# Moving tiles of the dense stages begin 32 bytes off the weights' tiles

## The reference

```
z = rms_norm(x) @ w_in;  zf, zq, zk, zv, zm = split(z)
y = concat(fourier(zf), window_attention(zq, zk, zv), memory_attention(zm, mem))
x = x + rms_norm(group_norms(y) @ w_out)
gate, up = split(rms_norm(x) @ w_ffn_in)          # 2 x 2816 channels
x = x + rms_norm((silu(gate) * up) @ w_ffn_out)
```

```
x = x + 0.5 * swiglu(rms_norm(x), ffn1_w1, ffn1_w2)
proj = rms_norm(x) @ w_in + b_in
x = x + (g0 * y_a(proj) + g1 * y_b(proj) + g2 * y_c(proj)) @ w_out
x = x + 0.5 * swiglu(rms_norm(x), ffn2_w1, ffn2_w2)
```

## Time and profile before

| | us | share |
|---|---|---|
| median of three runs | 3464.14 | |
| profiled execution, span | 3464.2 | |
| TensorE matmuls | 3364.4 | 97% |
| TensorE weight loads (beside matmuls) | 2886.5 | 83% |
| VectorE | 2451.1 | 71% |
| ScalarE | 1628.3 | 47% |
| GpSimd | 67.0 | 2% |

### The profile page before, as it was taken

The page is one execution under the profiler, slowest core; times in us unless marked ns, Lnnn a source line. Parts: engine busy times, 40 slices in busy tenths (PEclk is TensorE's granted clock), DMA queues, the critical chain, the costliest instruction groups (busy, mean ns, idle before and its releaser), DMA issues. The chain is left out here.

```text
span 3464.2 us, 49516 instructions
## 1 busy us (share of the span) xinstructions
PE 3364.4 (97%) x19557; PEld 2886.5 (83%) x19557; DVE 2451.1 (71%) x3500; ACT 1628.3 (47%) x2399; POOL 67.0 (2%) x96
## 2 busy tenths in 40 slices
PE   7999999999999999999999999999999989999999
PEld 5679988768998899887678899889988757788997
DVE  8669854759872988467885698458864888658863
ACT  4645643445652556335523365336542562335642
POOL 1000000000000000000000000000000000000000
PEclk9999999999999999999999999999999999999999
DMA  4123323213332333232132333333333212223332
GB/s 141 50 73 110 110 87 110 92 44 92 110 110 97 92 106 115 94 101 65 54 97 86 98 106 102 101 106 108 101 104 108 71 49 85 85 97 98 110 104 85
DMA packets 341371, 325.25 MB, mean 94 GB/s; under 512 B 31960, under 2 KB 312356, under 8 KB 341156
## 3 DMA queue, kind: packets, MB, share of 16 engines
q1 hardware_dynamic: 335588, 307.95, 28.0%
q0 software_dynamic: 3776, 12.45, 1.6%
q10 hardware_dynamic: 1792, 1.88, 0.2%
HBM read 313.84 MB, written 2.10 MB: 91 GB/s over the span
## 5 line engine op out<-in xcount | busy, mean ns | idle before, releaser
L2168 DVE TENSOR_TENSOR w_lo<-raw,w_hi 128x2048 fp32r<-128x2048 f32 x190 | 435.2, 2291 | 482.7 <-ACT w_hi L1524 482.4
L1524 ACT ACTIVATE w_hi<-raw 128x2048 fp32r<-128x2048 f32 x190 | 363.8, 1915 | 835.5 <-PE products L799 582.7
L799 PE MATMUL products<-a_hi,w_hi 128*128 128x512 f32 (+1 forms) x1216 | 489.6, 403 | 12.1 <-DVE a_lo L2228 9.5
L799 PE MATMUL products<-a_hi,w_lo 128*128 128x512 f32 (+1 forms) x1216 | 476.3, 392 | 0.0
L799 PE MATMUL products<-a_lo,w_hi 128*128 128x512 f32 (+1 forms) x1216 | 475.5, 391 | 0.0
L940 PE MATMUL products<-seven_x,w_hi 128*128 128x256 f32 x2592 | 464.5, 280 | 2.4 <-DVE w_lo L2467 2.3
L940 PEld LDWEIGHTS products<-seven_x,w_hi 128*128 128x128 f32 x2592 | 395.0, 188 | 4.1 <-DVE w_lo L2467 3.6
L940 PE MATMUL products<-seven_x,more_hi 128*128 128x256 f32 x1632 | 376.1, 280 | 5.6 <-ACT rs_b L1636 5.6
L940 PE MATMUL products<-seven_x,w_lo 128*128 128x256 f32 x1296 | 361.5, 279 | 0.0
L799 PEld LDWEIGHTS products<-a_hi,w_hi 128*128 128x128 f32 (+1 forms) x1216 | 229.3, 189 | 69.0 <-issue 16.5
L940 PEld LDWEIGHTS products<-seven_x,more_hi 128*128 128x128 f32 x1632 | 277.5, 188 | 6.8 <-ACT rs_b L1636 6.8
(11 more groups left out here) (465 smaller groups left out, 7242.8 us busy)
## 6 DMA issues: line engine op xcount, KB each, us to landing
raw<-in_ffn_w SPq DMA_DIRECT2D x244, 512.0 KB, 4.2
raw<-in_w_in SPq DMA_DIRECT2D x108, 512.0 KB, 4.6
raw<-in_w_ffn_in SPq DMA_DIRECT2D x88, 512.0 KB, 4.3
raw<-in_w_ffn_out SPq DMA_DIRECT2D x40, 512.0 KB, 4.5
raw<-in_w_out SPq DMA_DIRECT2D x32, 512.0 KB, 4.0
raw<-in_ffn_w SPq DMA_DIRECT2D x24, 384.0 KB, 3.6
x_sums<-x_sums POOLq DMA_DIRECT2D x12, 512.0 KB, 5.9
raw<-in_w_mem_kv SPq DMA_DIRECT2D x8, 512.0 KB, 3.9
```

Of the source, the lines that this page charges most:

```text
L799: mm = pe.matmul(G[pair][0:m, into + b, 0:n], w[:, s, at:at + m], x, start=(first or into > 0) and k == 0 and q == 0, stop=(last or ends) ...
L1524: act.activation(w_hi[:, s, :], raw[:, s, :], ACT.Copy).then_inc(hi_ready, 1)
L2168: dve.tensor_tensor(w_lo[:, s, :], raw[:, s, :], w_hi[:, s, :].bitcast(F32), ALU.subtract).then_inc(lo_ready, 1)
```

## The change

Three constants ODD_A, ODD_H and ODD_Y, all 32, move tiles:

- `a_hi` and `a_lo` begin 32 bytes behind their old places; the region's length is written out, so that REGION_B stays where it was.
- `h_hi`, `h_lo` and `h_full` (which shares h_lo's bytes) begin 32 bytes later; h_lo's region is 1 KB longer. The early weight forms of the block products, which lie near the region's end, move by 512 bytes.
- `m_hi`, `m_lo` and what follows them in the first mixer begin 32 bytes later.
- The branches begin at BRANCHES = REGION_B + 32, and with them REGION_T, so `ya`, `yb`, `yc`, `mg_hi`, `mg_lo`, `q_head`, `conv`, `gate_w` and the rest of the second mixer shift by 32 bytes.

No instruction, wait or transfer is added, removed or reordered; sizes and types stay.

```diff
+ODD_A, ODD_H, ODD_Y = 32, 32, 32
...
-    a_hi = place("a_hi", [P, DC, SEQ], F32R)
-    a_lo = place("a_lo", [P, DC, SEQ], F32R)
+    a_hi = place("a_hi", [P, DC, SEQ], F32R, at=REGION_A + ODD_A)
+    a_lo = place("a_lo", [P, DC, SEQ], F32R, at=REGION_A + 16 * KB + ODD_A)
+    top[0] = REGION_A + 32 * KB
...
-    h_hi = place("h_hi", [P, FC, SEQ], F32R)
-    top[0] += LINE
+    h_hi = place("h_hi", [P, FC, SEQ], F32R, at=REGION_B + ODD_H)
+    top[0] = REGION_B + 44 * KB + LINE
     H_LO = top[0]
-    h_lo = place("h_lo", [P, FC, SEQ], F32R)
+    h_lo = place("h_lo", [P, FC, SEQ], F32R, at=H_LO + ODD_H)
+    top[0] = H_LO + 45 * KB
...
-    early_hi = place("early_hi", [P, 3, QUAD], F32R, at=H_LO + 32 * KB)
+    early_hi = place("early_hi", [P, 3, QUAD], F32R, at=H_LO + 32 * KB + LINE)
...
-    h_full = place("h_full", [P, FC, SEQ], at=H_LO)
+    h_full = place("h_full", [P, FC, SEQ], at=H_LO + ODD_H)
...
+    b1[0] += ODD_H
     m_hi = in_b("m_hi", [P, DC, MEM], F32R)
...
-    b1[0] = REGION_B
+    BRANCHES = REGION_B + ODD_Y
+    b1[0] = BRANCHES
     yc_hi = in_b("yc_hi", [P, LC, SEQ], F32R)
...
-    gate_w = place("gate_w", [P, LC, 2, P], at=REGION_B + 44 * KB)
+    gate_w = place("gate_w", [P, LC, 2, P], at=BRANCHES + 44 * KB)
```

More of the change, by code:

```diff
@@ L320, in two_blocks @@
     more_lo = place("more_lo", [P, 5, QUAD], F32R, at=REGION_A + 10 * KB)
-    early_hi = place("early_hi", [P, 3, QUAD], F32R, at=H_LO + 32 * KB)
-    early_lo = place("early_lo", [P, 3, QUAD], F32R, at=H_LO + 38 * KB)
+    early_hi = place("early_hi", [P, 3, QUAD], F32R, at=H_LO + 32 * KB + LINE)
+    early_lo = place("early_lo", [P, 3, QUAD], F32R, at=H_LO + 38 * KB + LINE)
     more_sums = place("more_sums", [P, 5, QUAD], at=REGION_A + 10 * KB)
-    early_sums = place("early_sums", [P, 3, QUAD], at=H_LO + 38 * KB)
+    early_sums = place("early_sums", [P, 3, QUAD], at=H_LO + 38 * KB + LINE)
     x_sums = place("x_sums", [P, 11, 4 * HALF], at=REGION_B + ODD)
-    h_full = place("h_full", [P, FC, SEQ], at=H_LO)
+    h_full = place("h_full", [P, FC, SEQ], at=H_LO + ODD_H)
     X_SUMS = {"B11": 1, "T3": 3, "T2": 5, "B12": 6, "T4": 7, "B21": 8, "T1": 9, "B22": 10}
@@ L422, in two_blocks @@
     lru_in = in_b("lru_in", [P, LC, SEQ])
-    glu = place("glu", [P, LC, SEQ], at=REGION_B)
-    conv = place("conv", [P, LC, SEQ], at=REGION_B + 8 * KB)
+    glu = place("glu", [P, LC, SEQ], at=BRANCHES)
+    conv = place("conv", [P, LC, SEQ], at=BRANCHES + 8 * KB)
     craw_sq = place("craw_sq", [P, 5, SEQ], at=REGION_T)
-    lru_tmp = place("lru_tmp", [P, 3, SEQ], at=REGION_B + 26 * KB)
-    craw = place("craw", [P, 6, SEQ], at=REGION_B + 32 * KB)
-    gate_w = place("gate_w", [P, LC, 2, P], at=REGION_B + 44 * KB)
-    mla_prob.append(place("mla_prob4", [P, ROWS_4], at=REGION_B + 34 * KB))
+    lru_tmp = place("lru_tmp", [P, 3, SEQ], at=BRANCHES + 26 * KB)
+    craw = place("craw", [P, 6, SEQ], at=BRANCHES + 32 * KB)
+    gate_w = place("gate_w", [P, LC, 2, P], at=BRANCHES + 44 * KB)
+    mla_prob.append(place("mla_prob4", [P, ROWS_4], at=BRANCHES + 34 * KB))
     mla_prob.append(place("mla_prob5", [P, ROWS_4], at=REGION_T))
```

## The result

The changed kernel takes 3510.2 us, the median of four runs (3506.87 to 3511.57), against 3464.51 us (3461.09 to 3469.84): a ratio of 1.0131 [1.0117, 1.0145], slower by 45.7 us. The forecast was 3444 us; the first rival, "the offset takes the good pace away", is what happened, and its 3506 us (with L838) came close. All lines of the kernel stand five further down: L799 is now L804, L838 is L843, L940 is L945, L1201 is L1206, L1524 is L1529 and L2168 is L2173.

The account below looks back on a forecast made before the run. The prediction took TensorE, busy for 97% of the span, and its matmul pace as the bound. Sum: 3464.2 - 20.5 (L799) + 0 (all else) = 3444 us (-0.6%); 8 in 10 range 3436 to 3498 us.

Parts of the forecast that it names:

- the first rival: Dense 512-column matmuls of L799 lose their good pace: +31.9 us, 3496 us, or 3506 us if L838 follows; chance 0.32.
- Step (1): L799's 6144 matmuls of 512 columns, moving tiles 32 bytes later, gain 3.3 ns each: -20.5 us, bounds -20.5 to +31.9.
- The term of -20.5 us: The gain claimed for L799 in Step (1): 6144 matmuls of 512 columns at 3.3 ns each.
- The upper bound of 5.2 ns: Most that one L799 matmul of 512 columns was taken to lose, from weights off the raster: 231.9 - 226.7 ns.
- Step (3): Matmuls that fill the attention (L1201, 384, worth 1.3 us) and those of the heads (L1398): taken as 0.
- Steps (4) and (5): ScalarE and VectorE on tiles 32 bytes off, the DMA into gate_w and the moved early forms: cost 0.
- Step (2): By-token stages at L838, 1968 matmuls, only the stationary tile moved: bounds -6.6 to +10.2 us, taken as 0.
- The last rival: L838's 1968 matmuls lose up to 10.2 us while L799 gains 20.5: 3454 us, inside the forecast's range, no own chance.
- The second rival: Overhead at 512 columns isn't the two reads meeting, so the offset brings little or nothing: 3457 to 3471 us; chance 0.23.

Follow-up runs that it names:

- e1: The kernel before with only h_hi, h_lo and h_full 32 bytes off: 3483.49 us against 3466.74, ratio 1.0048.
- e5: The changed kernel with a at 64 bytes, h and m at 128, branches and mg at 256, block products at 64: 3487.51 us, before at 3464.0.
- e7: The kernel before with the block products' moving tiles at multiples of 512 too: 3496.14 us, ratio 1.009.
- e2: The kernel before with only m_hi, m_lo and what follows them in the first mixer 32 bytes off: 3465.52 us against 3466.74, ratio 0.9998.
- e12: The kernel before with block products and m at 192 bytes, every 512-column stage at 0: 3443.96 us against 3464.22, ratio 0.9937.
- e4: The kernel before with the weight chunks of the mixer's 160-column unit 256 columns apart in place of 160: 3466.97 us, one run.
- e6: The changed kernel with a at 256 bytes, h and m at 96, branches and mg at 384, block products at 96: 3515.66 us, before at 3464.0.

## Why the prediction was wrong

**Where it failed.** Step (1), in the sentence "the aligned overhead is the same 32 cycles at 256 and at 512 columns, so it looks like a cost per matmul and not per column". The sizes in it are right: 120.0 and 226.7 ns are 288 and 544 cycles. The inference is not. The best paces that any run showed are 113.3 ns at 256 columns and 226.7 ns at 512: 272 and 544 cycles, 17 for every 16 columns at both widths. What no displacement tried takes away grows with the columns, 16 cycles at 256 and 32 at 512. So the aligned stream of 256 columns carried 16 cycles that an offset can take away (32 bytes take 8), and the aligned stream of 512 carried none that any of them takes: it was at its best already, and every displacement off the raster of 256 bytes cost. Two numbers of equal size were taken for one cause. The term of -20.5 us came out as +40.6.

**What had spoken for the truth.** The rival's own evidence was the nearer row: the earlier trace rows was at 512 columns, the block products were not. Of what was held against it, "changes its displacement with every chunk, the edit has one throughout" was no reason, as 32 bytes throughout are slower still (233.3 ns in e1, 231.9 there). That the block products "go from 226.7 ns to 116.7 ns without any run-in" told nothing of 512 columns. The upper bound of 5.2 ns was too low by 1.4: it was read at displacements that are multiples of 128 bytes, and a steady 128 bytes cost less than 32 do (232.3 ns in e5, 233.3 in e1).

**What held.** That 32 bytes are worth 3.3 ns at 256 columns: on the memory's tiles, and the other way round in e7, where taking them from the block products costs 1.009 [1.0073, 1.0106]. Step (3) at nothing for L1206's memory products: e2. (Its 192 matmuls on a and those of the heads have 512 columns and lost about 5 ns each, under 2 us in all.) Steps (4) and (5) at nothing: the other engines' sums did not move, and idle time of TensorE, in which a slower split or a later transfer would show, fell by 7.0 us.

**The rest.** Step (2), L838 taken as 0, lost 13.0 us: a displacement of -32 is as bad as one of +32, beyond its bound of 10.2 us. The last rival, that L838 goes against L799, falls with it.

**The second rival and the page behind it.** "No change" rested on a matmul without a weight load beside it being only 1 ns shorter. That tells nothing of an offset: the loss of 6.6 ns is in a stream whose weight loads are the same. The Trainium skill, SBUF — State Buffer, section Who interferes with whom, lists TensorE's two read ports as independent. The measurements differ from what one would read out of that: the same instructions with only the distance between the two tiles changed take 1.0131 [1.0117, 1.0145] (after), 1.0048 (e1) and 1.009 (e7) of the time. No run shows why the distance counts, whether the two reads meet or something else; the runs show that it decides which paces there are, at 512 columns modulo 256 bytes.

## What to carry to other kernels

Where TensorE is the bound, read the step from start to start at each width, and compare it with the best step seen at that same width before calling the excess an overhead; a cost measured at one shape is moved to another only after checking which part of it grows with the shape. In fp32r, treat the displacement between the moving and the stationary tile as a parameter per width: here none at 512 columns and 192 bytes at 256, of which e12's profiled execution had the full gain in four of six long runs. Where a mean hides two paces, as at 64 bytes, look at each run by itself. An address sweep over several stages at once, read by pace and not by total time, costs one run per offset.

## What was not expected of the hardware

- A stream of fp32r matmuls has steady paces that go with the displacement: 226.7, 229.0 or 232.3 to 234.2 ns at 512 columns; from 113.3 to 120.0 at 256.
- The sign turns with the width: zero is the best displacement at 512 columns (226.7 ns, as at 256 bytes) and the worst at 256 columns (120.0 ns, as at 96 bytes).
- One displacement can have two steady paces: 113.3 and 117.7 ns in one execution, at 192 bytes (e12) and at 64 (e5).
- Blocks of 96 weight columns ran at 230.4 ns with chunks 256 bytes off the moving tile (e4), where blocks of 128 at that displacement ran at 226.7 (e6). Blocks of 96 at no displacement were not tried.
